# Summing the squares of the second norm on VectorE instead of TensorE

## The chip, the cores and the metric

The kernel runs on one core of one Trainium2 chip. The metric is the device time of one launch in microseconds (us). The kernel before took 2256.66 us, the median of 3 runs (2256.58 to 2256.97).

## The reference, cut to what matters

Two layers. Each has a sub-layer of three attention branches and a sub-layer of retrieved experts. Ahead of each stands an RMS norm with a modulation. The change is in the way from the first sub-layer into the second norm:

```python
def rms_norm(x, g):
    xf = x.astype(jnp.float32)
    y = xf * lax.rsqrt(jnp.mean(xf * xf, axis=-1, keepdims=True) + EPS)
    return (y * g.astype(jnp.float32)).astype(x.dtype)

# in each layer
x = x + g1 * parallel_mixers(h, w_in[l], ..., w_out[l])      # ends in merged @ w_out
h = rms_norm(x, norm2_g[l]) * (1.0 + sc2) + sh2
x = x + g2 * peer_ffn(h, w_query[l], ...)                    # begins with h @ w_query
```

x has 256 tokens of 1024 channels, all in float32.

## The kernel before, in words

Activations lie transposed: 128 partitions hold 128 channels of one chunk, and the free dimension is the 256 tokens. The 1024 channels are 8 chunks, so `x` is `[128, 8, 256]`. All weights come as one stream of tiles of 128 x 1024 floats, 684 of them, into four buffers `raw`. Each float32 product is made of three matmuls in a faster format: ScalarE rounds a tile to `hi` (`head`, L471), VectorE subtracts to get the rest `lo` (`rest_of`, L779), and TensorE adds up hi x hi, hi x rest and rest x hi (L1255 to L1257). Splitting runs three tiles ahead (`AHEAD = 3`): beside tile t the other two engines split tile t + 3. `hi` and `lo` have four buffers each, so a tile can be split only when the tile four before it has been multiplied.

The stage around the change is the output projection `w_out`, which I call the out stage: 8 weight tiles, one for each chunk of x. For each chunk k:

- TensorE multiplies 24 matmuls of 256 columns into `pj[k % 2]` (`project`, L1288 on) and signals `tile_done`. It may start only when `out_free` says that chunk k - 2 has left the same PSUM buffer.
- VectorE splits tile k + 3 (L779), waits for `tile_done`, and adds the product times the modulation onto `x[:, k, :]` (L1043), which signals `out_free`.
- ScalarE splits tile k + 3 (L471), waits for `out_free`, and squares `x[:, k, :]` into `sq2[:, k, :]` (L644), which signals `sq_ready`.
- TensorE, between the tiles, multiplies a matrix of ones with the squares of the chunk before (`squares`, L1280). That adds up the 128 channels of the chunk in every partition; the eight of them accumulate in one PSUM region, `wk[:, 0, 0:256]`. Each such product of plain float32 appears in the trace as two matmul records and two weight loads.

After the eighth, ScalarE takes the logarithm and the exponential of the sum (L499, L500), which is 1/root. VectorE scales chunk after chunk of x (L819), ScalarE rounds it (L505) and VectorE subtracts (L830). With the first chunk so prepared, TensorE starts on the query projection, the next 8 tiles.

Each engine runs its own instructions in the order in which the code stands; the order between engines is set by semaphores alone. The first norm of each layer adds up its squares in the same way (L514 and L1280), and is not touched.

Of the kernel before, what the change touches and what calls it, by code (L numbers as in the profile page):

```python
# [19 lines left out]
DEPTH, SEQ, D = 2, 256, 1024  # L20
P = 128
KC = D // P
# [12 lines left out]
N_OUT = KC  # L35
# [10 lines left out]
T_OUT = T_BR + N_BR  # L46
# [17 lines left out]
MG1, MS2, MC2, MG2, MS1, MC1 = (KC * n for n in range(6))  # L64
# [5 lines left out]
SPLIT = 4  # L70
AHEAD = 3
# [33 lines left out]
def trunk(nc, stream, par_dram, const_dram, mix_dram, taba_dram, keys_dram, front_dram, ada_dram, x_dram, out_dram):  # L105
    f32, f32r, u32 = mybir.dt.float32, mybir.dt.float32r, mybir.dt.uint32
    ALU, ACT, AX = mybir.AluOpType, mybir.ActivationFunctionType, mybir.AxisListType

    ctx = ExitStack()
    with ctx:  # L110
        def sb(name, shape, dt=f32):
            return ctx.enter_context(nc.sbuf_tensor(name, shape, dt))

        def sem(name):
            return ctx.enter_context(nc.semaphore(name))
# [5 lines left out]
        x = sb("x", [P, KC, SEQ])  # L121
# [9 lines left out]
        mod = sb("mod", [P, N_ADA])  # L131
# [12 lines left out]
        ones = const[:, C_ONE:C_ONE + P]  # L144
# [12 lines left out]
        def part(n):  # L157
            a = flat[:, used[0]:used[0] + n]
            used[0] += n
            return a  # L160
# [41 lines left out]
        sq2 = part(KC * SEQ).rearrange("p (k s) -> p k s", s=SEQ)  # L202
# [14 lines left out]
        pj = [ctx.enter_context(nc.psum_tensor(f"pj{i}", [P, 512], f32)) for i in range(2)]  # L217
        wk = ctx.enter_context(nc.psum_tensor("wk", [P, 6, 512], f32))
# [36 lines left out]
        tile_done = sem("tile_done")  # L255
        out_free = sem("out_free")
        x_ready = sem("x_ready")
        sq_ready = sem("sq_ready")
        ss_ready = sem("ss_ready")
        rstd_ready = sem("rstd_ready")  # L260
        h_ready = sem("h_ready")
# [505 lines left out]
        def _(dve):  # L767
# [7 lines left out]
            def rest_of(t, j):  # L775


                dve.wait_ge(hi_done, t + 1)
                nc.vector.tensor_tensor(lo[j % SPLIT][:, :], raw[j % RAW][:, :], hi[j % SPLIT][:, :].bitcast(f32),  # L779
                                        ALU.subtract).then_inc(lo_done, 1)  # L780
# [24 lines left out]
            with dve.Fori(0, DEPTH) as l:  # L805
# [3 lines left out]
                L0 = l * TILES  # L809
# [6 lines left out]
                def norm(n, sq):  # L816

                    def scaled(k):
                        nc.vector.scalar_tensor_tensor(sq[:, k, :], x[:, k, :], amp[:, n, k:k + 1], rstd, ALU.mult,  # L819
                                                       ALU.mult).then_inc(h_ready, 1)  # L820

                    dve.wait_ge(rstd_ready, 2 * l + n + 1)
                    scaled(0)
                    for k in range(KC):
                        if k + 1 < KC:
                            scaled(k + 1)
                        shift = (MS1, MS2)[n] + k

                        dve.wait_ge(h_hi, l * HI_READY + ((0, HI_2)[n] + k + 1))
                        nc.vector.scalar_tensor_tensor(mov_lo[:, k, :], sq[:, k, :], mod[:, shift:shift + 1],  # L830
                                                       mov_hi[:, k, :].bitcast(f32), ALU.add,
                                                       ALU.subtract).then_inc(mov_ready, 1)
# [174 lines left out]
                with dve.Fori(0, 3) as br:  # L1007

                    dve.wait_ge(sigmoids, 3 * l + br + 1)
                    for j in range(4):  # L1010
                        t = L0 + br * 4 + (T_BR + j)
# [22 lines left out]
                nc.vector.scalar_tensor_tensor(amp[:, 1, :], mod[:, MC2:MC2 + KC], 1.0, par[:, PG2:PG2 + KC],  # L1034
                                               ALU.add, ALU.mult)

                with dve.Fori(0, N_OUT // 4) as i:
                    for j in range(4):
                        t = L0 + i * 4 + (T_OUT + j)
                        rest_of(t + AHEAD, j + AHEAD)  # L1040
                        dve.wait_ge(tile_done, t + 1 + SPLIT)
                        xk = x[:, bass.ds(i * 4 + j, 1), :].squeeze(1)
                        nc.vector.scalar_tensor_tensor(xk, pj[j % 2][:, 0:SEQ], mod[:, bass.ds(i * 4 + (MG1 + j), 1)],  # L1043
                                                       xk, ALU.mult, ALU.add).then_inc(out_free, 1)
                norm(1, sq2)
                with dve.Fori(0, N_QUERY // 4) as i:
                    for j in range(4):
# [20 lines left out]
                for u in range(17):  # L1068
# [7 lines left out]
                    if done is not None:  # L1076
# [4 lines left out]
                                                           v[:, 0, :].unsqueeze(2).to_broadcast([P, 16, 16]),  # L1081
                                                           v[:, 1, :].unsqueeze(1).to_broadcast([P, 16, 16]), ALU.add))
                    first = [step(nc.vector.max(v8[:, 0:8], sc)) for sc, _, v8, _ in halves]
                    split_early(1)
                    if done is not None:
# [11 lines left out]
                    if halves:  # L1097
                        dve.wait_ge(dve_step, removed[1])
                        second = [step(nc.vector.max(v8[:, 8:16], r)) for _, r, v8, _ in halves]
# [3 lines left out]
                    for sc, _, v8, i8 in halves:  # L1103
                        nc.vector.max_index(i8[:, 0:8], v8[:, 0:8], sc)
# [114 lines left out]
                with dve.Fori(0, ADA_LATE // 4) as i:  # L1219
                    for j in range(12):  # L1220
                        down_group(i * 3 + (LATE_AT // 4 + j // 4), j % 4)
                        if j % 3 == 2:

                            k = j // 3
# [5 lines left out]
                t = L0 + TILES - 4  # L1230
# [21 lines left out]
        def _(pe):  # L1252
# [16 lines left out]
            for k in range(KC):  # L1269
                last = pe.matmul(wkf[:, 2048 + k * P:2048 + (k + 1) * P], c_silu[:, k:k + 1].to_broadcast([P, P]), ident,  # L1270
                                 start=True, stop=True)
            last.then_inc(c_spread, 1)

            with pe.Fori(0, DEPTH) as l:
                L0 = l * TILES

                def squares(n, sq, k):

                    pe.wait_ge(sq_ready, 2 * KC * l + (n * KC + k + 1))
                    last = pe.matmul(wk[:, 0, 0:SEQ], ones, sq[:, k, :], start=k == 0, stop=k == KC - 1)  # L1280
                    if k == KC - 1:
                        last.then_inc(ss_ready, 1)

                def project(t, j, o, bank, chunks=None, at=range(KC), between=None):

                    pe.wait_ge(lo_done, t + 1)  # L1288
                    pe.wait_ge(out_free, l * OUTS + o + 1)
                    for k in range(KC):  # L1290
                        if chunks is not None:
                            pe.wait_ge(mov_ready, l * M_READY + (chunks + k + 1))
                        if between is not None and k == KC // 2:
                            between()
                        last = product(pj[bank][:, 0:SEQ], *chunk(j, k), mov_hi[:, at[k], :], mov_lo[:, at[k], :],
                                       k == 0, k == KC - 1)
                    return last
# [167 lines left out]
                for n in range(N_BR):  # L1465
                    br, j = n // 4, n % 4
# [9 lines left out]

                for k in range(N_OUT):
                    project(L0 + (T_OUT + k), k, O_OUT + k, k % 2, None if k else M_MERGED, MERGED_AT).then_inc(tile_done, 1)
                    if k:
                        squares(1, sq2, k - 1)  # L1480
                squares(1, sq2, KC - 1)
                wait_alone(pe, rstd_ready, 2 * l + 2)
                def key_scores(h):
# [207 lines left out]
```

## Time and profile before

| what | value |
|---|---|
| median of 3 runs | 2256.66 us |
| the profiled execution, its own time | 2254.9 us |
| its span, first to last instruction | 2253.1 us |
| TensorE (PE) busy | 2185.6 us, 97% |
| VectorE (DVE) busy | 1658.4 us, 74% |
| ScalarE (ACT) busy | 1219.1 us, 54% |
| mean granted TensorE clock | 0.987 |

The profile comes from one execution, whose time is 1.8 us under the median. Times in the trace are counted from the start of the span. The out stage of the first layer lies at 287.7 to 316.5 us, that of the second at 1396 to 1425.1 us. Matmuls overlap in the records (a record of 0.28 us, the next one 0.12 us later), so what a group of them costs TensorE is read from start to start. A granted clock of 1.00 is 2.4 GHz, one of 0.50 is 1.2 GHz.

### The profile page before, as it was taken

What the parts mean: (1) busy time and instruction counts of PE and PEld (TensorE: products, weight loads), DVE (VectorE), ACT (ScalarE), POOL (GpSimd) and SP (SyncE); (2) the same over time, 40 slices, a digit from 0 to 9 for tenths busy, and PEclk for the clock granted to TensorE, in tenths of its full rate; (3) what the DMA queues carried; (4) which work ended last, traced back from release to release, by engine and by line L of the source; (5) the groups of instructions that cost most, each with busy time, mean ns of one, the idle gap of its engine ahead of it and who ended that gap; (6) DMA issues with size and microseconds to landing.
All of it is one profiled execution on the core that took longest, in us unless ns stands there. A gap on an engine that the chain in (4) does not pass through costs nothing.

```text
span 2253.1 us, 45818 instructions
## 1 busy us (share of the span) xinstructions
PE 2185.6 (97%) x15268; PEld 2027.8 (90%) x15268; DVE 1658.4 (74%) x3159; ACT 1219.1 (54%) x2152; POOL 272.2 (12%) x300
## 2 busy tenths in 40 slices
PE   4999989999999999999989999999999999999998
PEld 4899989999999988888888999899999999888887
DVE  6777755889689956777557768478894998567765
ACT  3556554444567655445555564544445776554454
POOL 0220000000157500000002100000001773000000
PEclk8999999999999999999999999999999999999999
DMA  8456644555533357776544665445555333578764
GB/s 322 169 197 211 211 157 151 179 185 176 188 132 113 111 195 248 257 259 229 193 178 169 211 217 200 133 158 185 181 175 190 117 112 131 194 266 257 257 213 163
DMA packets 114454, 427.51 MB, mean 190 GB/s; under 512 B 12704, under 2 KB 12960, under 8 KB 113056
## 3 DMA queue, kind: packets, MB, share of 16 engines
q1 hardware_dynamic: 114336, 426.08, 55.6%
q8 instruction: 56, 0.92, 0.2%
q14 instruction: 62, 0.51, 0.1%
HBM read 424.98 MB, written 1.05 MB: 189 GB/s over the span
## 4 chain that ended last, share of the span: by engine, by line
PE 92%; DVE 2%; issue 2%; DMA 2%; ACT 1%; POOL 0%; SPq 0%; DVEq 0%; ACTq 0%; POOLq 0%
PE pj L1255 17%; PE pj L1256 17%; PE pj L1257 17%; PE wk L1255 10%; PE wk L1256 10%; PE wk L1257 10%; PE wk L1546 5%; DMA arena<-in_front 1%; PE wk L1351 1%; DMA arena<-in_ada 1%; ACT hi L471 1%; PE wk L1328 1%; PE wk L1306 1%; PE wk L1344 1%; PE wk L1493 0%
## 5 line engine op out<-in xcount | busy, mean ns | idle before, releaser
L779 DVE TENSOR_TENSOR lo<-raw,hi 128x1024 fp32r<-128x1024 f32 x683 | 840.9, 1233 | 508.9 <-ACT hi L471 501.1
L1255 PE MATMUL pj<-mov_hi,hi 128*128 128x256 f32 x3376 | 987.7, 293 | 35.8 <-DVE mov_lo L830 26.8
L471 ACT ACTIVATE hi<-raw 128x1024 fp32r<-128x1024 f32 x683 | 721.0, 1057 | 453.2 <-PE wk L1257 345.0
L1256 PE MATMUL pj<-mov_lo,hi 128*128 128x256 f32 x3376 | 959.7, 284 | 0.0
L1257 PE MATMUL pj<-mov_hi,lo 128*128 128x256 f32 x3376 | 959.6, 284 | 0.0
L1255 PEld LDWEIGHTS pj<-mov_hi,hi 128*128 128x128 f32 x3376 | 651.0, 193 | 50.6 <-DVE mov_lo L830 28.8
L1256 PEld LDWEIGHTS pj<-mov_lo,hi 128*128 128x128 f32 x3376 | 652.8, 193 | 0.5
L1257 PEld LDWEIGHTS pj<-mov_hi,lo 128*128 128x128 f32 x3376 | 651.7, 193 | 0.0
L1255 PE MATMUL wk<-hi,mov_hi 128*128 128x512 f32 x1024 | 398.6, 389 | 1.7 <-DVE mov_lo L1204 1.7
L1256 PE MATMUL wk<-lo,mov_hi 128*128 128x512 f32 x1024 | 398.4, 389 | 0.0
L1257 PE MATMUL wk<-hi,mov_lo 128*128 128x512 f32 x1024 | 398.3, 389 | 0.0
L459 POOL TENSOR_SCALAR mov_hi<-const,routes 128x128 fp32r<-128x128 f32 x256 | 218.2, 867 | 1039.3 <-DVE gateT L1156 909.3
L1255 PEld LDWEIGHTS wk<-hi,mov_hi 128*128 128x128 f32 x1024 | 192.2, 188 | 42.0 <-DVE mov_lo L1204 2.1
L1256 PEld LDWEIGHTS wk<-lo,mov_hi 128*128 128x128 f32 x1024 | 192.2, 188 | 39.8
L1257 PEld LDWEIGHTS wk<-hi,mov_lo 128*128 128x128 f32 x1024 | 192.2, 188 | 39.8
L677 ACT ACTIVATE arena<-pj 128x256 f32 (+1 forms) x192 | 73.7, 384 | 282.8 <-PE pj L1257 282.7
L1168 DVE TENSOR_SCALAR onehot_a<-const,routes,gateT 128x128 f32<-128x128 f32 x512 | 146.9, 350 | 0.0
L784 DVE SCALAR_TENSOR_TENSOR arena<-arena,silu_c 128x1024 f32<-128x1024 f32 x88 | 106.8, 1223 | 8.6 <-DMA arena<-in_ada 5.9
L1204 DVE TENSOR_TENSOR mov_lo<-arena,mov_hi 128x256 fp32r<-128x256 f32 x256 | 106.5, 417 | 1.1 <-ACT mov_hi L739 1.1
L739 ACT ACTIVATE mov_hi<-arena 128x256 fp32r (+1 forms) x256 | 101.9, 400 | 0.0
L704 ACT ACTIVATE mov_lo<-const,routes 128x128 fp32r<-128x128 f32 x256 | 81.0, 397 | 0.0
L521 ACT ACTIVATE arena<-pj 128x256 f32<-128x256 f32 x62 | 23.7, 383 | 93.9 <-PE pj L1257 93.8
(170 smaller groups left out, 1478.0 us busy)
## 6 DMA issues: line engine op xcount, KB each, us to landing
raw<-in_stream SPq DMA_DIRECT2D x684, 512.0 KB, 3.3
arena<-in_ada SPq DMA_DIRECT2D x72, 512.0 KB, 4.7
onehot_a<-in_ada SPq DMA_DIRECT2D x24, 512.0 KB, 4.6
arena<-in_front SPq DMA_DIRECT2D x4, 2048.0 KB, 18.6
arena<-in_taba SPq DMA_DIRECT2D x2, 1536.0 KB, 19.1
arena<-in_keys SPq DMA_DIRECT2D x2, 1024.0 KB, 6.1
x<-in_xT SPq DMA_DIRECT2D x1, 1024.0 KB, 4.9
arena<-in_mix SPq DMA_DIRECT2D x2, 512.0 KB, 15.3
```

The costliest lines, as they stand in the source:

```text
L459: e = nc.gpsimd.tensor_scalar(onehot_b[0][:, quad % 4 * 2 + r, :], iota, idx2T[:, t:t + 1], None, ALU.is_equal)
L471: nc.scalar.activation(hi[j % SPLIT][:, :], raw[j % RAW][:, :], ACT.Copy).then_inc(hi_done, 1)
L704: e = nc.scalar.activation(onehot_b[1][:, slot + r, :], iota, ACT.Abs, bias=idx2T[:, quad * 4 + r:quad * 4 + r + 1], scale=-1.0)
L739: nc.scalar.activation(w_hi[:, s, :], group_of(n), ACT.Copy).then_inc(w_head, 1)
L779: nc.vector.tensor_tensor(lo[j % SPLIT][:, :], raw[j % RAW][:, :], hi[j % SPLIT][:, :].bitcast(f32), ALU.subtract).then_inc(lo_done, 1)
L784: nc.vector.scalar_tensor_tensor(tile, tile, 1.0, silu_c[:, :], ALU.mult, ALU.mult, accum_out=col)\
L1168: e = nc.vector.tensor_scalar(onehot_a[:, quad % 2 * 4 + r, :], iota, idx1T[:, t:t + 1], gateT[:, t:t + 1], ALU.is_equal, ALU.mult)
L1204: nc.vector.tensor_tensor(w_lo[:, s, :], group_of(n), w_hi[:, s, :].bitcast(f32), ALU.subtract).then_inc(w_rest, 1)
L1255: pe.matmul(out, w_h, m_h, start=first, stop=False)
L1256: pe.matmul(out, w_h, m_l, start=False, stop=False)
L1257: return pe.matmul(out, w_l, m_h, start=False, stop=last)
L1546: last = pe.matmul(wk[:, 2 + quad % 4, :].rearrange("p (i t) -> p t i", t=4)[:, r, :], onehot_a[:, quad % 2 * 4 + r, :], onehot_b[half][:, ...
```

## The change

In the out stage VectorE adds the squares of the chunks up, in place, in `sq2[:, 0, :]`: six additions of 128 x 256 in each layer, for the squares of chunks 1 to 6 onto those of chunk 0. Each stands behind the split of a tile and ahead of the update of x. With chunk 0 that makes seven chunks in one sum. TensorE multiplies ones with this sum, and then with the squares of chunk 7 alone. So of eight products with ones two are left, and both stand behind the last tile. A new semaphore `sq_sum` orders the additions. VectorE's loop of two turns of four is written out as eight steps. The first norm stays as it is, and so do ScalarE's, GpSimd's and the DMA queue's instructions.

```diff
+        sq_sum = sem("sq_sum")
...
-                with dve.Fori(0, N_OUT // 4) as i:
-                    for j in range(4):
-                        t = L0 + i * 4 + (T_OUT + j)
-                        rest_of(t + AHEAD, j + AHEAD)
-                        dve.wait_ge(tile_done, t + 1 + SPLIT)
-                        xk = x[:, bass.ds(i * 4 + j, 1), :].squeeze(1)
-                        nc.vector.scalar_tensor_tensor(xk, pj[j % 2][:, 0:SEQ], mod[:, bass.ds(i * 4 + (MG1 + j), 1)],
-                                                       xk, ALU.mult, ALU.add).then_inc(out_free, 1)
+                for k in range(N_OUT):
+                    t = L0 + (T_OUT + k)
+                    rest_of(t + AHEAD, k + AHEAD)
+                    if k >= 2:
+
+                        dve.wait_ge(sq_ready, 2 * KC * l + KC + k)
+                        if k > 2:
+                            dve.wait_ge(sq_sum, (KC - 2) * l + k - 2)
+                        nc.vector.tensor_tensor(sq2[:, 0, :], sq2[:, 0, :], sq2[:, k - 1, :], ALU.add).then_inc(sq_sum, 1)
+                    dve.wait_ge(tile_done, t + 1 + SPLIT)
+                    nc.vector.scalar_tensor_tensor(x[:, k, :], pj[k % 2][:, 0:SEQ], mod[:, MG1 + k:MG1 + k + 1],
+                                                   x[:, k, :], ALU.mult, ALU.add).then_inc(out_free, 1)
...
                 for k in range(N_OUT):
                     project(L0 + (T_OUT + k), k, O_OUT + k, k % 2, None if k else M_MERGED, MERGED_AT).then_inc(tile_done, 1)
-                    if k:
-                        squares(1, sq2, k - 1)
+
+                pe.wait_ge(sq_sum, (KC - 2) * l + KC - 2)
+                pe.matmul(wk[:, 0, 0:SEQ], ones, sq2[:, 0, :], start=True, stop=False)
                 squares(1, sq2, KC - 1)
```

VectorE in the out stage before, two steps of the loop (`lo` and `raw` are the split tile, `x` the updated chunk):

```order
L779 TENSOR_TENSOR lo1<-raw1,hi1 128x1024 [waits hi_done]
L1041 REGISTER_ALU
L1043 ISA [waits tile_done]
L1043 SCALAR_TENSOR_TENSOR x<-pj0,mod,x 128x256
L779 TENSOR_TENSOR lo2<-raw2,hi2 128x1024 [waits hi_done]
L1041 REGISTER_ALU
L1043 ISA [waits tile_done]
L1043 SCALAR_TENSOR_TENSOR x<-pj1,mod,x 128x256
```

The same engine and place in the changed kernel, the steps of chunks 2 and 3 (its lines are numbered one to five higher; `arena<-arena` is the addition):

```order
L780 TENSOR_TENSOR lo1<-raw1,hi1 128x1024 [waits hi_done]
L1046 TENSOR_TENSOR arena<-arena 128x256 [waits sq_ready]
L1047 REGISTER_ALU
L1048 SCALAR_TENSOR_TENSOR x<-pj0,mod,x 128x256 [waits tile_done]
L780 TENSOR_TENSOR lo2<-raw2,hi2 128x1024 [waits hi_done]
L1046 TENSOR_TENSOR arena<-arena 128x256 [waits sq_sum,sq_ready]
L1047 REGISTER_ALU
L1048 SCALAR_TENSOR_TENSOR x<-pj1,mod,x 128x256 [waits tile_done]
```

An addition now stands between the split and the update of x.

TensorE before, at the end of the out stage's last tile and the start of the query projection (`pj` is a tile's product, `wk<-arena,const` the product with ones, here those of the squares of chunks 6 and 7):

```order
L1256 MATMUL pj1<-mov_lo,hi3 128x256
L1257 MATMUL pj1<-mov_hi,lo3 128x256
L1279 REGISTER_ALU
L1280 MATMUL wk<-arena,const 128x256 [waits sq_ready] x2
L1288 REGISTER_ALU [waits rstd_ready]
L1289 REGISTER_ALU [waits lo_done]
L1292 REGISTER_ALU [waits out_free]
L1255 MATMUL pj0<-mov_hi,hi0 128x256 [waits mov_ready]
```

The same in the changed kernel:

```order
L1261 MATMUL pj1<-mov_lo,hi3 128x256
L1262 MATMUL pj1<-mov_hi,lo3 128x256
L1485 ISA
L1486 MATMUL wk<-arena,const 128x256 [waits sq_sum]
L1285 MATMUL wk<-arena,const 128x256 [waits sq_ready]
L1293 REGISTER_ALU [waits rstd_ready]
L1294 REGISTER_ALU [waits lo_done]
L1297 REGISTER_ALU [waits out_free]
L1260 MATMUL pj0<-mov_hi,hi0 128x256 [waits mov_ready]
```

Here two products stand before and two now, the first of which waits for VectorE's last addition. The six others, which stood between the tiles, are gone.

## Rows read from the trace of the kernel before

**Rows 1.** The page: busy us (share) and instructions, three engines.

```profile
PE 2185.6 (97%) x15268; PEld 2027.8 (90%) x15268; DVE 1658.4 (74%) x3159; ACT 1219.1 (54%) x2152; POOL 272.2 (12%) x300
```

**Rows 2.** Waits of VectorE, then of ScalarE, at 288 to 316 us: total, times, longest.

```profile
DVE lo L779 <- ACT hi L471: 11.4, 7, 1.8
...
ACT arena L644 <- DVE x L1043: 15.5, 8, 2.4
```

**Rows 3.** Timeline of VectorE: start us, us, instruction [idle before <- releaser].

```profile
287.20 2.77 DVE L1027 TENSOR_TENSOR mov_lo<-arena,mov_hi 128x256 fp32r<-128x256 f32 x8 [0.28 <-DVE arena L1021]
...
290.42 0.17 DVE L1034 SCALAR_TENSOR_TENSOR amp<-mod,par 128x8 f32<-128x8 f32 x1
290.69 1.23 DVE L779 TENSOR_TENSOR lo<-raw,hi 128x1024 fp32r<-128x1024 f32 x1
...
297.13 1.22 DVE L779 TENSOR_TENSOR lo<-raw,hi 128x1024 fp32r<-128x1024 f32 x1 [1.62 <-ACT hi L471]
298.28 0.48 DVE L1043 SCALAR_TENSOR_TENSOR x<-pj,mod,x 128x256 f32 x1
300.38 1.23 DVE L779 TENSOR_TENSOR lo<-raw,hi 128x1024 fp32r<-128x1024 f32 x1 [1.62 <-ACT hi L471]
301.52 0.48 DVE L1043 SCALAR_TENSOR_TENSOR x<-pj,mod,x 128x256 f32 x1
...
314.60 0.48 DVE L1043 SCALAR_TENSOR_TENSOR x<-pj,mod,x 128x256 f32 x1
```

**Rows 4.** Timeline of ScalarE in the same stage.

```profile
298.98 0.42 ACT L644 ACTIVATE arena<-x  x1 [1.88 <-DVE x L1043]
299.30 1.04 ACT L471 ACTIVATE hi<-raw 128x1024 fp32r<-128x1024 f32 x1
```

**Rows 5.** The chain that ended last, 1418 to 1431 us: start us, us, what.

```profile
1418.86 0.43 PE wk L1280 x2
1419.29 0.12 PE pj L1255
...
1422.04 0.13 PE pj L1257
1422.17 0.03 issue
...
1423.93 0.42 ACT arena L644
1424.36 0.04 issue
1424.40 0.71 PE wk L1280 x2
```

**Rows 6.** One line by form: L1027's instructions, duration min/median/max.

```profile
L1027 DVE TENSOR_TENSOR mov_lo<-arena,mov_hi x16: 415/417/424, 287.2 to 1398.2; 128x256 fp32r<-128x256 f32 x16
```

**Rows 7.** Stretches: us, busy (x) of PE, PEld, DVE, ACT, POOL, clock, DMA share, GB/s.

```profile
284.00:288.00 4.00, 1.67 (x14) 1.47 (x13) 3.46 (x7) 2.44 (x8) 0.00 (x0) 1.00 0.71 230
313.50:316.60 3.10, 1.13 (x4) 0.33 (x3) 1.58 (x2) 0.51 (x2) 0.00 (x0) 1.00 0.44 152
317.00:317.20 0.20, 0.00 (x0) 0.00 (x0) 0.00 (x0) 0.19 (x1) 0.00 (x0) 0.94 1.29 532
323.00:324.00 1.00, 1.00 (x6) 0.91 (x5) 0.82 (x3) 0.72 (x3) 0.00 (x0) 0.50 0.00 0
324.00:325.00 1.00, 1.00 (x8) 0.83 (x8) 0.54 (x2) 0.85 (x1) 0.00 (x0) 1.00 0.00 0
1140.00:1142.00 2.00, 2.00 (x6) 1.63 (x5) 0.00 (x0) 0.26 (x1) 0.31 (x1) 0.50 0.96 369
1426.20:1426.60 0.40, 0.00 (x0) 0.00 (x0) 0.40 (x2) 0.00 (x0) 0.00 (x0) 0.88 0.00 0
```

**Rows 8.** Timeline of TensorE: products with ones between tiles, and at 1141 us.

```profile
313.33 0.60 PE L1280 MATMUL wk<-arena,const 128*128 128x256 f32 x2
...
1141.23 1.06 PE L1280 MATMUL wk<-arena,const 128*128 128x256 f32 x2
```

**Rows 9.** The chain again, 320.8 to 322 us, in the query projection.

```profile
320.86 0.37 PE pj L1255
321.22 0.21 PE pj L1256
321.44 0.21 PE pj L1257
321.65 0.36 PE pj L1255
```

## The prediction

> **What bounds the kernel now.** I read the page first: TensorE is busy 97% of the span, VectorE 74% [rows 1]. That invites the thought that each product with ones taken from TensorE is a gain. So I went to the stage that is changed, and read who waits there. In the out stage ScalarE waits for VectorE's update of x before each of its eight squarings, 15.5 us in all, and VectorE waits for ScalarE's rounding before seven of its eight splits, 11.4 us in all [rows 2]. Neither waits for TensorE. The two timelines show why. VectorE: the split starts at 297.13, the update of x follows 1.15 us later (298.28) with no gap, and the next split starts at 300.38 [rows 3]. ScalarE: the squaring at 298.98, 0.70 us after the update began; the rounding of the next tile 0.32 us after that (299.30) [rows 4]; and the next split 1.08 us after that (300.38). This is a closed ring: update of x(k), squaring k, rounding of tile k + 4, split of tile k + 4, update of x(k+1). 0.70 + 0.32 + 1.08 + 1.15 = 3.25 us for a turn, and the starts of two updates, 298.28 and 301.52, are 3.24 us apart. Nothing in the ring is idle for another reason.
>
> TensorE in the same stage: a tile takes 2.88 us (1419.29 to 1422.17), a product with ones 0.43 us [rows 5]; together 3.31 us, nearly the same pace as the ring. Both look full. Which of them ends the stage is seen at its end. The last tile of the first layer is done at 313.33, where its product with ones follows [rows 8]; the last update of x starts at 314.60 [rows 3], 1.3 us later. It was not waiting for the tile but standing behind its split. In the second layer the tile is done at 1422.17, and the last squaring starts at 1423.93 [rows 5]; less the 0.70 us of the ring that is an update at 1423.23, 1.1 us late. Then come squaring, product, root and the first scaled chunk, one behind the other, and TensorE waits for all of it. So the ring sets the end of the stage.
>
> **The products that go.** Six products with ones leave each layer, 6 x 0.43 = 2.6 us of TensorE [rows 5]. TensorE's pace falls from 3.31 to 2.88 us a tile, but it was not what ended the stage; it reaches the end earlier and waits longer. Worth: 0. If the end hung on it, it would be 2.6 us a layer; that is a rival below.
>
> **The additions that come.** Each is float32, 128 x 256, two operands in SBUF. Instruction L1027 has just this shape, 417 ns [rows 6], but what counts is from start to start. Eight of them take 2.77 us, so (2.77 - 0.42) / 7 = 0.336 us each [rows 3], with waits and register steps between them. The split and the update behave alike: 1.15 us from start to start where the split lasts 1.23. The addition stands behind the split and ahead of the update, inside the ring. VectorE is idle for 1.6 us in each turn, but ahead of the split, where it waits for ScalarE; the addition comes after that wait, so the idle time doesn't hide it. Its own waits are met: the square of chunk k - 1 was made on ScalarE ahead of the rounding for which the split has just waited, and the addition before it is a turn old. Behind the addition stand the update, and for that the squaring, the next rounding and the next split. So each addition lengthens its turn by its whole spacing: 6 x 0.336 = 2.02 us a layer. Bounds: 0.336, and 0.46 if the addition's whole duration (0.417) and one gap of 0.04 us, like those in the chain [rows 5], counted. That is 2.0 to 2.75 us a layer; I take the lower end, since the row that it rests on has waits too.
>
> The Trainium skill (VectorE: DVE Perf Modes, The DRAIN you can't avoid) says that after each VectorE instruction the next does not start until the pipeline is empty. By that rule six additions would cost at least 6 x 0.417 = 2.5 us a layer, 1.0 us more over both. The rows here speak against it: instructions start 0.08 us before the one ahead ends.
>
> **The loop written out.** In the second half of the stage the turn across the loop's end costs 0.2 us more, but on ScalarE's side, whose loop stays. At the entry 0.27 us lie between L1034 and the first split, of which L1034 takes 0.17 [rows 3]. A start without the loop's two entry instructions may save up to that 0.1 us plus the overlap of 0.08. I take -0.10 us a layer (0 to -0.18).
>
> **TensorE's new wait.** The product with the sum waits for the sixth addition. The addition ends about as the last update starts; the squaring that the other product needs ends 0.70 + 0.42 us after that, so the sum's product, 0.7 us, is out of the way. Behind it on TensorE stands only the last product. It costs nothing by itself. But TensorE idles longer ahead of it. Counting with the ring's new turn of 3.58 us, updates start at 291.84 and 295.03 as before, then at 298.6, 302.2, 306.0, 309.5, 313.1 and 316.6. A tile may start when the update two before it is over: tile 5 at 302.7, tile 6 at 306.5, tile 7 at 310.0, ending at 312.9. Between them lie pauses of 0.6 to 0.9 us, and after tile 7 one of 3.8 us, up to the sum's product at 316.7; the last product starts at 317.8, 4.9 us behind the last tile.
>
> The granted clock bears on that. Before, it was still 1.00 at the last product (mean of 313.5 to 316.6) and fell in 317.0 to 317.2 and in 1426.2 to 1426.6 [rows 7], which is 3.9 us and 4.2 us behind the ends of the last tiles, although a product lay between. With 4.9 us the last product probably meets the low clock, 1.2 GHz. At 1140 to 1142 the clock was 0.50 [rows 7] and one product of two records took 1.06 us, against 0.70 before here [rows 5, 8]: +0.36 us a layer. Bounds: 0 if the clock holds, 0.46 if the start is also slower. I take 0.36. [...]
>
> After the norm TensorE works at 0.50 until 324 [rows 7] but is held back by the chunks, which come every 0.79 us (320.86 to 321.65), while its three matmuls need 0.64 there [rows 9]. The clock costs little before the eighth chunk. If it came back a microsecond later than now, 0.5 us a layer would be lost; I take 0 and keep that for the range.
>
> **The sum.** Per layer 2.02 - 0.10 + 0.36 = 2.28; two layers 4.56 us. The profiled execution took 2254.9 (span 2253.1 and 1.8 around it) and would take 2259.5. The median of the runs is 1.8 above that execution, so I add the sum to it: 2256.66 + 4.56 = 2261.2 us. A difference under 0.2%, 4.5 us, can't be told from none in this kernel; my sum lies on that edge.
>
> **Rivals.**
> - The clock falls inside the out stage. With pauses of 0.6 to 0.9 us in 3.6, tiles at half clock take 24 x 0.21 = 5.1 us [rows 9]. From tile 5 on: 302.7 + 3 x 5.1 = 318.0, so the last update starts at 318.1, not 316.6: +1.5 us a layer, 2264.2 us. Where it decides: the low level by tile 5; from tile 6 on it is only 0.2 us. For it: less work in the stage than before. Against it: at 284 to 288 TensorE was busy for 1.67 of 4 us, with one pause above 2 us, and the clock stayed 1.00 [rows 7]. Chance 0.10.
> - The additions cost their whole duration and a gap: 12 x 0.46 = 5.5 in place of 4.0, 2262.7 us. For it: an instruction with two waits stands nowhere back to back in the rows that I used. Chance 0.14.
> - The additions are mostly covered, because the ring has play that I do not see (an update that could come late without delaying the squaring): only the end effects are left, 2 x 0.26 = 0.5 us, 2257.2 us. For it: VectorE idles half of each turn. Against it: ScalarE's waits end with the update every time [rows 2]. Chance 0.08.
> - TensorE sets the end of the stage after all. Then six products less are 2 x 2.6 = 5.2 us of gain, 2251.5 us. For it: the chain that ended last runs through TensorE's tile and product in the second layer [rows 5], and 97% busy. It decides if the ring's turn is under 2.88 us; it is measured at 3.24, and longer with the addition. Chance 0.05.
>
> My forecast has the rest, 0.63, and its own range is 2259.8 to 2262.4. The range of 2258.8 to 2264.0 takes in the second rival and part of the first, and leaves out the fourth and most of the third. Slower by over 0.2% (above 2261.2): half of the forecast's 0.63 and both costly rivals, about 0.53. Faster: 0.05. Same: the rest, 0.42.
>
> **What would show it.** In the profile after, the updates of chunks 2 to 7 should start 3.58 us apart (3.78 across ScalarE's loop end), and the last one 2.0 us later than before when counted from the stage's first split; the addition should start 1.15 us behind the split and the update 0.34 us behind the addition. TensorE should wait for `out_free` from tile 5 on and for the last addition 3.8 us; the last product should be a record of about 1.06 us at a clock of 0.50. VectorE should still never wait for TensorE's tile. I am wrong if the updates keep 3.24 us, if TensorE shows no new waits in the stage, or if the clock reads 0.50 between its tiles.

## The result, and the profile after

Twelve runs of each kernel on the same chips: 2258.76 us (2255.94 to 2260.57) after, 2254.78 us (2248.61 to 2257.96) before. The ratio is 1.0018, with a 95% interval of 1.0011 to 1.0026: the change makes the kernel slower by about 4 us (2.5 to 5.9). The sum said +4.6 us, of the same sign. As a difference to the 2256.66 us that the forecast was built on, the range was +2.1 to +7.3 us, the narrower one of the forecast alone +3.1 to +5.7, and +4.0 lies in both. As an absolute time, 2258.76 us stands on the lower edge of the range (2258.8) and 2.4 us under the forecast 2261.2; 1.9 us of that come from the base, a median of three runs, since over twelve the kernel before has 2254.8. A ratio of 1.0018 is just under the 0.2% that I had called the edge of what can be told (a change of none is still outside the interval).

The page after, busy us (share) and instructions of each engine; it answers to [rows 1]:

```profile
PE 2183.9 (97%) x15244; PEld 2024.0 (90%) x15244; DVE 1662.8 (74%) x3171; ACT 1219.1 (54%) x2152; POOL 272.2 (12%) x300
```

TensorE has 24 matmul records less (12 products of two records each) and VectorE 12 instructions more. The shares say nothing on which of them counts.

The timeline of VectorE after, the steps of chunks 2 and 3, against [rows 3] (the two ends of the ring stand with it):

```profile
290.38 0.48 DVE L1048 SCALAR_TENSOR_TENSOR x<-pj,mod,x 128x256 f32<-128x256 f32 x1 [0.54 <-PE pj L1262]
...
295.68 1.23 DVE L780 TENSOR_TENSOR lo<-raw,hi 128x1024 fp32r<-128x1024 f32 x1 [1.62 <-ACT hi L472]
296.82 0.42 DVE L1046 TENSOR_TENSOR arena<-arena 128x256 f32<-128x256 f32 x1
297.16 0.48 DVE L1048 SCALAR_TENSOR_TENSOR x<-pj,mod,x 128x256 f32<-128x256 f32 x1
299.26 1.23 DVE L780 TENSOR_TENSOR lo<-raw,hi 128x1024 fp32r<-128x1024 f32 x1 [1.62 <-ACT hi L472]
300.40 0.42 DVE L1046 TENSOR_TENSOR arena<-arena 128x256 f32<-128x256 f32 x1
300.74 0.48 DVE L1048 SCALAR_TENSOR_TENSOR x<-pj,mod,x 128x256 f32<-128x256 f32 x1
...
315.15 0.48 DVE L1048 SCALAR_TENSOR_TENSOR x<-pj,mod,x 128x256 f32<-128x256 f32 x1
```

The addition starts 1.14 us behind the split, the update 0.34 us behind the addition, and two updates are 3.58 us apart (297.16 to 300.74) where they were 3.24. VectorE still waits 1.62 us for ScalarE in each turn: the idle time was not used up, it was moved along.

Who waited in TensorE's queue after, 288 to 332 us (line waited for: total us, times, longest):

```profile
PE wk L1486 <- DVE arena L1046: 3.6, 1, 3.6
PE pj L1260 <- DVE mov_lo L831: 2.6, 1, 2.6
PE pj L1260 <- DVE x L1048: 0.6, 2, 0.4
```

Before, in the same stretch, TensorE had one wait at the end of the stage, that for the last squaring:

```profile
PE wk L1280 <- ACT arena L644: 1.8, 1, 1.8
```

What TensorE saved came back as waiting: for the sixth addition and, ahead of its last two tiles, for updates of x. Its last products in the first layer, and the clock beside them (the columns of [rows 7]):

```profile
315.28 1.22 PE L1486 MATMUL wk<-arena,const 128*128 128x256 f32 x2 [3.60 <-DVE arena L1046]
316.31 1.22 PE L1285 MATMUL wk<-arena,const 128*128 128x256 f32 x2
```

```profile
316.00:317.00 1.00, 1.00 (x4) 0.50 (x2) 0.00 (x0) 0.25 (x1) 0.00 (x0) 0.50 0.86 303
```

Both products ran at 1.2 GHz. In the second layer the clock held a little longer, and the last product took 0.80 us:

```profile
1429.94 0.80 PE L1285 MATMUL wk<-arena,const 128*128 128x256 f32 x2 [0.33 <-ACT arena L645]
```

To compare kernels I cut the stage at four events: its first matmul, the first and the last update of x, and the logarithm. From there to the query projection's first matmul it is 2.55 us in every kernel. All in us from the profiles, first layer / second layer:

| kernel | first matmul to first update | first to last update | last update to logarithm | first matmul to query projection |
|---|---|---|---|---|
| before | 4.16 / 4.16 | 22.76 / 22.74 | 1.90 / 1.90 | 31.38 / 31.35 |
| after | 4.61 / 4.67 | 24.77 / 24.77 | 2.42 / 1.99 | 34.35 / 33.99 |
| products_only | 4.43 / 4.44 | 22.76 / 22.76 | 2.14 / 2.11 | 31.88 / 31.87 |
| additions_only | 3.98 / 4.49 | 24.78 / 24.77 | 2.42 / 2.42 | 33.73 / 34.24 |
| additions_first | 4.66 / 4.67 | 22.77 / 22.76 | 2.42 / 2.42 | 32.41 / 32.40 |
| additions_twice | 3.99 / 4.50 | 26.79 / 26.78 | 2.42 / 2.42 | 35.76 / 36.26 |
| fillers | 3.98 / 3.98 | 24.79 / 24.78 | 1.90 / 1.90 | 33.23 / 33.22 |
| update_first | 4.52 / 4.83 | 22.97 / 22.66 | 1.91 / 1.91 | 31.96 / 31.96 |
| update_first_sum | 4.67 / 3.17 | 20.14 / 20.16 | 1.90 / 1.91 | 29.27 / 27.80 |
| before_again | 4.15 / 4.63 | 22.77 / 22.76 | 1.90 / 1.89 | 31.37 / 31.83 |
| before_third | 4.15 / 4.83 | 22.76 / 22.77 | 1.90 / 1.89 | 31.36 / 32.05 |

Between the two profiles of before and after the stages take 2.97 and 2.64 us more, 5.6 in all, while the spans differ by 3.9 (2253.1 and 2257.0). The other 1.7 us lie in stretches whose code is the same; I take them for the scatter of single executions.

### The profile page after: what moved, and what is told of

Read it like the earlier page. It is cut to its first block, busy times and chain, and to the rows that moved or that the text cites. A ratio compares the mean times of both kernels' runs of the same rounds, so it can differ in the third digit from the quotient of the medians.

```text
span 2257.0 us, 45762 instructions
## 1 busy us (share of the span) xinstructions
PE 2183.9 (97%) x15244; PEld 2024.0 (90%) x15244; DVE 1662.8 (74%) x3171; ACT 1219.1 (54%) x2152; POOL 272.2 (12%) x300
## 4 chain that ended last, share of the span: by engine, by line
PE 92%; DVE 3%; issue 2%; ACT 1%; DMA 1%; POOL 0%; SPq 0%; ACTq 0%; DVEq 0%; POOLq 0%
PE pj L1260 17%; PE pj L1261 17%; PE pj L1262 17%; PE wk L1260 10%; PE wk L1261 10%; PE wk L1262 10%; PE wk L1552 5%; DMA arena<-in_front 1%; PE wk L1356 1%; ACT hi L472 1%; PE wk L1311 1%; PE wk L1349 1%; DVE mov_lo L831 0%; PE wk L1333 0%; PE wk L1499 0%
```

## The experiments

**products_only and additions_only: the change in two halves.** The first leaves VectorE's additions out, the second keeps all products and adds into a tile of its own.

```diff
 # products_only
-                    if k >= 2:
-                        dve.wait_ge(sq_ready, 2 * KC * l + KC + k)
-                        ...
-                        nc.vector.tensor_tensor(sq2[:, 0, :], sq2[:, 0, :], sq2[:, k - 1, :], ALU.add).then_inc(sq_sum, 1)
...
-                pe.wait_ge(sq_sum, (KC - 2) * l + KC - 2)
+                pe.wait_ge(sq_ready, 2 * KC * l + (KC + 1))
 # additions_only
+        acc = part(SEQ)
...
-                        nc.vector.tensor_tensor(sq2[:, 0, :], sq2[:, 0, :], sq2[:, k - 1, :], ALU.add).then_inc(sq_sum, 1)
+                        nc.vector.tensor_tensor(acc, acc if k > 2 else sq2[:, 0, :], sq2[:, k - 1, :], ALU.add).then_inc(sq_sum, 1)
...
-                pe.wait_ge(sq_sum, (KC - 2) * l + KC - 2)
-                pe.matmul(wk[:, 0, 0:SEQ], ones, sq2[:, 0, :], start=True, stop=False)
+                    if k:
+                        squares(1, sq2, k - 1)
```

> The changed kernel without VectorE's twelve additions: TensorE multiplies ones with the squares of chunk 0 and of chunk 7 alone, so the mean of the second norm leaves out chunks 1 to 6. Ring theory (ScalarE and VectorE set the stage): the six products less are worth nothing. From the first to the last update of x 22.75 us a layer, as before; the total within 0 to +1 us of before (up to 0.5 us a layer if the last product meets the low clock). Rival, TensorE sets the stage: 5.2 us faster than before.

> The twelve additions of the change, but into a tile that nothing reads, and all eight products with ones on TensorE as before. Ring theory: first to last update of x 24.77 us a layer (+2.02), the total +4.0 us, and the last product at full clock. Rival, additions cost their whole duration and a gap: 25.5 us a layer and +5.5 in all. Rival, additions are covered: 22.75 us and no change.

products_only: ratio to before 0.9998 (0.9990 to 1.0007). Twelve products less on TensorE brought nothing, and 5.2 us of gain (0.9977) is excluded. The ring kept 22.76 us. TensorE turned its saving into one long wait; its timeline at the end of the stage:

```profile
311.21 0.60 PE L1480 MATMUL wk<-arena,const 128*128 128x256 f32 x2
314.95 0.94 PE L1279 MATMUL wk<-arena,const 128*128 128x256 f32 x2 [3.14 <-ACT arena L645]
```

additions_only: ratio 1.0016 (1.0008 to 1.0025), the ring 24.78 and 24.77 us. So the additions alone make the change's whole cost; the rival of full durations (25.5 us) falls, and so does that of covered ones. One expectation missed: the last product met the low clock here too (2.42 us to the logarithm), although all products stood between the tiles. It stood behind a wait of 2.87 us where before it was 1.84; the longer ring makes the wait longer, and fillers, below, tests whether the wait makes the clock fall:

```profile
313.88 0.70 PE L1286 MATMUL wk<-arena,const 128*128 128x256 f32 x2
317.45 1.22 PE L1286 MATMUL wk<-arena,const 128*128 128x256 f32 x2 [2.87 <-ACT arena L646]
```

**additions_twice: the slope.**

```diff
+        acc = part(SEQ)
...
                         nc.vector.tensor_tensor(sq2[:, 0, :], sq2[:, 0, :], sq2[:, k - 1, :], ALU.add).then_inc(sq_sum, 1)
+                        nc.vector.tensor_tensor(acc, sq2[:, k - 1, :], sq2[:, k - 1, :], ALU.add)
```

> The changed kernel with a second addition of the same shape behind each of the twelve, into a tile that nothing reads. Ring theory: each adds its spacing of 0.336 us again, 26.8 us from the first to the last update, the total +4 us over the change, some +8 over before. Rival, the change's cost is not in the additions but in the end and the clock: 24.8 us and no more than the change.

Ratio 1.0035 (1.0022 to 1.0048), +7.9 us. The ring took 26.79 and 26.78 us: 0, 6 and 12 additions a layer give 22.76, 24.77 and 26.79, a straight line of 0.336 us for each. The timeline of VectorE shows each addition's start 0.33 to 0.34 us behind the one ahead of it, although it lasts 0.42:

```profile
297.21 0.42 DVE L1047 TENSOR_TENSOR arena<-arena 128x256 f32<-128x256 f32 x1
297.55 0.42 DVE L1048 TENSOR_TENSOR arena<-arena 128x256 f32<-128x256 f32 x1
297.88 0.48 DVE L1050 SCALAR_TENSOR_TENSOR x<-pj,mod,x 128x256 f32<-128x256 f32 x1
```

**additions_first: the same work, elsewhere in the step.**

```diff
                 for k in range(N_OUT):
                     t = L0 + (T_OUT + k)
-                    rest_of(t + AHEAD, k + AHEAD)
                     if k >= 2:
                         ...
                         nc.vector.tensor_tensor(sq2[:, 0, :], sq2[:, 0, :], sq2[:, k - 1, :], ALU.add).then_inc(sq_sum, 1)
+                    rest_of(t + AHEAD, k + AHEAD)
```

> The changed kernel with each addition moved ahead of the split of its step, into the 1.6 us in which VectorE waits for ScalarE's rounding. Ring theory: the addition is out of the ring, turns of 3.24 us, 22.75 us from the first to the last update, the total 0 to +1 us of before. Rival, an addition costs wherever it stands: 24.8 us and about +4.

Ratio 0.9995 (0.9986 to 1.0004). The ring is back at 22.77 and 22.76 us. The addition now waits for the squaring and is over before ScalarE's rounding is:

```profile
297.18 0.48 DVE L1048 SCALAR_TENSOR_TENSOR x<-pj,mod,x 128x256 f32<-128x256 f32 x1
298.33 0.42 DVE L1045 TENSOR_TENSOR arena<-arena 128x256 f32<-128x256 f32 x1 [0.67 <-ACT arena L645]
299.28 1.22 DVE L780 TENSOR_TENSOR lo<-raw,hi 128x1024 fp32r<-128x1024 f32 x1 [0.52 <-ACT hi L472]
```

One line moved takes the 4 us away. The cost was the place of the additions, not the additions. In this profile both layers had the low clock in the stage's first tile and at its end, so its stages are 1.0 us longer than before. The profiled execution took 2258.5 us, 4.6 above the median of its kernel, and the ratio doesn't show that.

**fillers: the pause and the clock.** Seven idle products on TensorE between the last tile and the wait for the sum.

```diff
+                for n in range(7):
+                    pe.matmul(wk[:, 1, 0:SEQ], ones, const[:, 0:SEQ], start=True, stop=True)
                 pe.wait_ge(sq_sum, (KC - 2) * l + KC - 2)
```

> The changed kernel with seven products of ones and constants in each layer on TensorE between the last tile and the wait for the sum, into a PSUM bank that nothing reads: 3.0 us of the 3.6 us pause. If the pause is what lowers the clock: 1.90 us from the last update to the logarithm in both layers (2.42 and 1.99 in the change), the ring unchanged at 24.77 us, the total 0 to -1 us of the change. Rival, the low clock comes by chance or from the stage's thinner work: 2.4 us again.

1.90 us from the last update to the logarithm in both layers, with the ring unchanged. With the pause left in, the same step was longer in all ten layers profiled (the change and the first four experiments). So the pause lowers the clock, and the low clock costs up to 0.52 us at this place. The stage's thinner work alone does not: update_first_sum, below, has the same two products, a wait of only 0.8 us ahead of the last one, and 1.90 and 1.91 us for the step. The rows of the fillers and of the last product (0.70 us again), and the clock over them:

```profile
311.86 3.19 PE L1486 MATMUL wk<-const 128*128 128x256 f32 x14
315.63 0.70 PE L1488 MATMUL wk<-arena,const 128*128 128x256 f32 x2 [0.59 <-DVE arena L1046]
316.66 0.70 PE L1285 MATMUL wk<-arena,const 128*128 128x256 f32 x2 [0.33 <-ACT arena L645]
```

```profile
315.00:317.40 2.40, 1.44 (x5) 0.59 (x4) 0.97 (x3) 0.42 (x2) 0.00 (x0) 1.00 0.35 116
```

The ratio to before, 1.0014 (1.0005 to 1.0023), is no test of it: 0.6 us is under what the runs can tell.

**update_first and update_first_sum: the ring opened.** If a ring of update, squaring, rounding and split sets the stage, taking the update out from behind the split must open it. The first does so in the kernel before, the second in the change.

```diff
 # update_first: the kernel before
-                        rest_of(t + AHEAD, j + AHEAD)
                         dve.wait_ge(tile_done, t + 1 + SPLIT)
                         ...
                                                        xk, ALU.mult, ALU.add).then_inc(out_free, 1)
+                        rest_of(t + AHEAD, j + AHEAD)
 # update_first_sum: the changed kernel
-                    rest_of(t + AHEAD, k + AHEAD)
                     if k >= 2:
                         ...
                                                    x[:, k, :], ALU.mult, ALU.add).then_inc(out_free, 1)
+                    rest_of(t + AHEAD, k + AHEAD)
```

> The kernel before with one edit: in the out stage VectorE updates x(k) ahead of the split of tile k + 3, not behind it. Ring theory: the ring is opened, since the update no longer waits for a split, and TensorE sets the stage at 3.31 us a tile (23.2 us from first to last update, but the first one earlier); the last update stands within 0.3 us of the end of the last tile where it stood 1.1 to 1.3 us behind it; -1.0 us a layer, -2.0 in all. Rival, the split comes too late in turn and TensorE waits for it: no gain.

> The changed kernel with the split of each step moved behind the update (order: addition, update, split). Ring theory: now TensorE sets the pace, 2.88 us a tile without products with ones between, 20.2 us from the first to the last update, the last product at full clock; -3.6 us a layer, -7 us against before and some -11 against the change. Rival, the twelve additions cost 4 us wherever they stand: -3 against before.

update_first: ratio 0.9997 (0.9988 to 1.0006). The gain of 2.0 us is not seen; it is not excluded either. The mechanism came as expected, VectorE now waits for TensorE's tile at every update, and TensorE for nobody between the tiles (VectorE's waits, 287 to 318 us, then a row of its timeline):

```profile
DVE x L1042 <- PE pj L1257: 13.3, 8, 1.7
```

```profile
314.13 0.48 DVE L1042 SCALAR_TENSOR_TENSOR x<-pj,mod,x 128x256 f32 x1 [1.68 <-PE pj L1257]
```

Two things are missing from the forecast. First, -1.0 us a layer was too much even at full clock: the turn of 3.30 us is longer than the ring's 3.24, and only the start gains. With a first update after 3.17 us (update_first_sum, second layer) and seven turns of 3.30, the last one stands at 26.3 us instead of 26.9; that is an estimate of -0.65 us a layer. Second, a stage paced by TensorE also pays the whole price of a low clock at its start. In this profile the first update came 4.52 and 4.83 us after the first matmul, against 4.16 before, and the stages came out 0.6 us longer. In the ring that delay is partly absorbed, because the first update stands behind a split anyway. How often the other executions met the low clock, and so why their median gained nothing, is not shown.

update_first_sum: ratio 0.9973 (0.9964 to 0.9982), 6.1 us faster than the kernel before and the fastest here. The products are now worth what they take: 20.14 and 20.16 us from first to last update, 2.88 us a turn, TensorE's pace without products. The interval, -8.1 to -4.1 us, leaves out the rival's -3. Of the 3.6 us a layer that I had expected, the second layer shows 3.55 (31.35 to 27.80) and the first, with the low clock in its first tile, 2.1. The additions are still twelve and cost nothing:

```profile
298.13 0.42 DVE L1045 TENSOR_TENSOR arena<-arena 128x256 f32<-128x256 f32 x1
299.48 0.48 DVE L1047 SCALAR_TENSOR_TENSOR x<-pj,mod,x 128x256 f32<-128x256 f32 x1 [0.93 <-PE pj L1262]
```

Against update_first, whose only difference beside the unrolled loop is the change itself, that is 5.4 us by the two ratios (0.9997 and 0.9973), 5.7 by the means of eleven runs each, and 5.3 by the first to last updates of both layers (45.63 and 40.30 us). The same change costs 4 us in one order of two instructions and brings 5 in the other.

**before_again and before_third: is the clock at the entry the kernel's?** In the first pair of profiles the clock was full throughout the stage's first tile before, and half for most of it after, in both layers.

> The kernel before, unchanged, for another profile. In its first profile the clock was high as the out stage began in both layers (4.16 us from the stage's first matmul to the first update), in the change's low in both (4.61 and 4.67, with 0.2 us saved by the loop written out). Theory that the clock at the entry differs between executions of the same code: one of the two new profiles shows a layer with a low clock there, some 4.6 to 4.8 us. Rival, it is a property of the changed kernel: 4.16 again in all layers. The ring 22.75 us in both.

> As the run ahead of it: the kernel before, unchanged. The clock at the out stage's entry low in one layer or more of the two new profiles if it differs between executions; high in all if it belongs to the kernel.

The second layer had the low clock in its first tile in both new profiles (4.63 and 4.83 us to the first update). The row of before_again, 1396 to 1399 us:

```profile
1396.00:1399.00 3.00, 3.00 (x18) 3.00 (x18) 2.63 (x9) 1.75 (x2) 0.00 (x0) 0.60 0.23 37
```

So the kernel before meets the low clock there too, and of the change's 5.6 us in the first pair of profiles I count the 0.45 and 0.51 us at the entry as chance. That the changed kernel meets it no more often is not shown: three profiles of the kernel before have it in two of six layers, the one of the change in both. It can't weigh much in the medians, since additions_first has the changed kernel's way into the stage, met the low clock there in both layers of its profile, and its ratio is 0.9995 (up to 1.0004).

## Why the prediction was right

- **What bounds the stage.** The ring of ScalarE and VectorE. Shown from both sides: products_only (nothing gained) and update_first_sum (the gain appears once the ring is open).
- **Six products less are worth 0.** Right, by products_only. The fourth rival, TensorE as the bound, falls; 97% busy and a chain that passes through TensorE were no evidence for it, since TensorE waited 1.8 us for the last squaring.
- **Six additions cost 2.02 us a layer.** Measured 24.77 less 22.76 and 22.74, 2.01 and 2.03. The lower bound was the right one: waits that are met cost nothing, also two in one instruction. The second rival (0.46 each) falls by the slope of 0.336, and so does the price of whole durations that the prediction took from the Trainium skill (VectorE: DVE Perf Modes, The DRAIN you can't avoid). It left out that the same passage goes on to say that an instruction which is not held back starts earlier; with that exception the page agrees with the spacing of 0.336 us against a duration of 0.417.
- **The last product at a low clock, 0.36 us a layer.** Right in kind, off in size: 0.52 in the first layer, 0.09 in the second, 0.61 in all where the sum had 0.72, and 0.52 lies above the bound of 0.46. The whole of it is the length of the last product: 1.22 and 0.80 us against 0.70. I had taken 1.06 from a product in the middle of a row of them at the low clock; why one behind the pause takes 1.22 is open. The sum's product, slow too in the first layer, cost nothing, as I had said: the last product started 1.16 us behind the last update (316.31 and 315.15, 1429.94 and 1428.78), as it did in additions_only (317.45 and 316.29), which has no such product, and 1.17 before.
- **The loop written out, -0.10 us a layer.** Measured -0.17 where the clock was high at the entry: 3.98 and 3.99 (additions_only, additions_twice, fillers) against 4.16 and 4.15. In the profile after, the first update waited for the tile instead, so the saving can't be read there.
- **The clock at the entry** was no term of the sum. Between executions of one kernel it moves the first update by up to 0.7 us a layer (4.15 to 4.83).
- **The first rival, a low clock from tile 5 on,** did not come. The clock was low in the first tile, and then read 1.00 from 291 us to the last tile's end, also where TensorE paused (the row below the list, after). TensorE waited ahead of two tiles, not three, because the slow first tile had made it later: in fillers, whose first tile was fast, it waited ahead of three, 1.2 us in all. For the same reason the first update waited 0.54 us for TensorE, the one wait of VectorE in the stage where I had forecast none; in fillers there was none.
- **The wait for the sixth addition** was 3.60 us, forecast 3.8.
- **The chance of "slower by over 0.2%"** was added up wrongly: half of 0.63 and the 0.10 and 0.14 of the costly rivals make 0.56, not 0.53.

The clock in the middle of the stage after, 306 to 309 us:

```profile
306.00:309.00 3.00, 2.63 (x22) 2.43 (x21) 1.96 (x3) 0.80 (x2) 0.00 (x0) 1.00 0.46 172
```

Ring, end and loop together make 4.04 + 0.61 - 0.34 = 4.3 us by the profiles, against 4.56 forecast and 4.0 (2.5 to 5.9) measured. What lies behind the stage was taken at 0, and was: from the logarithm to ScalarE's first copy of the scores that follow the query projection 10.72 and 10.80 us before, 10.72 and 10.71 after. In other executions it was up to 11.22 us (fillers, update_first; 11.13 in before_third), which is the 0.5 us a layer that the prediction kept for its range. The interval alone would not tell these sums apart; the mechanism is shown by the experiments, not by the closeness of the total. What stays open is how often the low clock reaches the last products. In the five profiles of kernels with a longer pause ahead of them (the change and the first four experiments; in additions_first it is two waits, 1.1 and 2.1 us, with a product between) the last step was longer in all ten layers, by 0.52 us in seven and by 0.09 to 0.24 in three.

## What to carry to other kernels

A busy share of 97% doesn't make an engine the one that ends a stage. Look for the ring: start from the instruction whose end lets the next stage begin, and walk back through who released whom until the same line comes again. If the walk never touches the busiest engine, work taken from it was worth nothing here, and work added in the ring cost its full spacing, even on an engine that idles half of each turn. Then try the order of instructions inside the ring before the amount of work: here moving one line changed the sign of the same change.

## What the runs showed of the hardware that I had not expected

- VectorE's additions of 128 x 256 float32 cost 0.336 us each from start to start over 0, 6 and 12 of them, though one lasts 0.417; it did not matter whether an instruction carried no, one or two met waits (the second additions of additions_twice have none; the turns into chunks 2 and 3 of the changed kernel, whose additions carry one and two, were both 3.58 us).
- The same code runs the out stage's first tile at 2.4 GHz in some executions and most of it at 1.2 GHz in others, after the same pause of 2.3 us (the second layer of before and of before_again). In a stage paced by TensorE the first update came 3.17 us after the first matmul with the one and 4.67 with the other (update_first_sum, its two layers); in the ring the difference was 0.5 to 0.7 us (additions_only, before_third).
